# A two-block transformer forward pass: the wait for the last x tile ahead of GpSimd's constant loads is taken out

## What is computed

```python
def hybrid_layer(x, layer_idx, w_in, w_s, b_s, a_ln_g, ...):
    h = jnp.einsum('bsd,de->bse', x, w_in)
    ...
    out_a = gmlp_mixer(a_u, a_v, w_s, b_s, a_ln_g, a_ln_b)
    lam = (jnp.exp(jnp.sum(lam_q1 * lam_k1)) - jnp.exp(jnp.sum(lam_q2 * lam_k2)) + lam_init)
    out_b = diff_attention(b_q, b_k, b_v, lam, lam_init, subln_g)
    out_c = dsa_attention(c_q, c_k, c_v, i_q, i_k, i_w)
    ...

def hybrid_layer_2(x, c, w_ada, b_ada, ...):
    mod = jax.nn.silu(c) @ w_ada + b_ada
    ...
```

## Time and profile before

| | |
|---|---|
| median of three runs (3083.93 to 3088.55) | 3087.78 us |
| time of the profiled execution | 3087.78 us |
| its span, first to last instruction | 3086.0 us |
| outside the span | 1.78 us |
| TensorE busy | 2963.2 us, 96% |
| granted TensorE clock, mean over the span | 0.987 |

### The profile page before, as it was taken

The page is one execution under the profiler, slowest core; times in us unless marked ns, Lnnn a source line. Parts: engine busy times, 40 slices in busy tenths (PEclk is TensorE's granted clock), DMA queues, the critical chain, the costliest instruction groups (busy, mean ns, idle before and its releaser), DMA issues.

```text
span 3086.0 us, 33232 instructions
## 1 busy us (share of the span) xinstructions
PE 2963.2 (96%) x13502; PEld 2200.6 (71%) x13509; DVE 1339.8 (43%) x2012; ACT 631.8 (20%) x1056; POOL 1388.8 (45%) x814
## 2 busy tenths in 40 slices
PE   9999989889999999999999889999998999999997
PEld 5444447467888888888888556667667888887886
DVE  0699957636432236243406652112214422334233
ACT  1501046512010001111301561101112211111111
POOL 2000000055666657656677004344445666566653
PEclk9999999999999999999999999999999999999998
DMA  4011146132332333433433002342333333333331
GB/s 114 21 41 41 34 118 171 56 139 88 96 107 92 103 96 92 128 94 96 123 90 95 1 1 62 82 140 77 83 113 92 95 97 95 96 96 123 94 98 61
DMA packets 364919, 273.22 MB, mean 89 GB/s; under 512 B 14048, under 2 KB 334816, under 8 KB 364768
## 3 DMA queue, kind: packets, MB, share of 16 engines
q1 hardware_dynamic: 357568, 253.30, 28.3%
q10 hardware_dynamic: 4720, 10.68, 0.9%
q0 software_dynamic: 2480, 7.13, 0.9%
HBM read 262.59 MB, written 8.49 MB: 88 GB/s over the span
## 4 chain that ended last, share of the span: by engine, by line
PE 88%; DVE 4%; DMA 3%; issue 2%; POOL 2%; ACT 1%; SPq 0%; DVEq 0%; ACTq 0%; POOLq 0%
PE PS L811 39%; PE PS L823 25%; PE PS L763 5%; PE PS L777 4%; PE PS L446 3%; DMA ring<-in_w_in 2%; PE PS L1015 2%; PE PS L883 2%; PE PS L464 2%; PE PS L484 2%; POOL w_low L1885 1%; PE PS L476 1%; PE PS L897 1%; DVE arena L552 1%; PE PS L978 1%
## 5 line engine op out<-in xcount | busy, mean ns | idle before, releaser
L1885 POOL TENSOR_TENSOR w_low<-ring,w_high 128x1024 fp32r<-128x1024 f32 x382 | 938.1, 2456 | 31.8
L1882 POOL TENSOR_SCALAR w_high<-ring 128x1024 fp32r<-128x1024 f32 x382 | 425.4, 1114 | 1023.4 <-PE PS L823 369.8
L823 PE MATMUL PS<-w_high,hid_high 128*128 128x512 f32 x864 | 337.2, 390 | 9.1 <-issue 9.1
L823 PE MATMUL PS<-w_high,hid_low 128*128 128x512 f32 x864 | 336.8, 390 | 0.0
L823 PE MATMUL PS<-w_low,hid_high 128*128 128x512 f32 x864 | 336.7, 390 | 0.0
L811 PE MATMUL PS<-hT_high,w_high 128*128 128x512 f32 x656 | 272.5, 415 | 14.3 <-POOL w_low L1885 14.3
L811 PE MATMUL PS<-x1T_high,w_high 128*128 128x512 f32 x704 | 275.1, 391 | 3.5 <-DVE x1T_low L1576 3.5
L811 PE MATMUL PS<-x1T_low,w_high 128*128 128x512 f32 x704 | 274.5, 390 | 0.0
L811 PE MATMUL PS<-x1T_high,w_low 128*128 128x512 f32 x704 | 274.4, 390 | 0.0
L811 PE MATMUL PS<-hT_high,w_low 128*128 128x512 f32 x656 | 257.5, 392 | 0.0
L811 PE MATMUL PS<-hT_low,w_high 128*128 128x512 f32 x656 | 257.2, 392 | 0.0
(11 more groups left out here) (268 smaller groups left out, 4602.0 us busy)
## 6 DMA issues: line engine op xcount, KB each, us to landing
ring<-in_w_ff SPq DMA_DIRECT2D x128, 512.0 KB, 3.8
ring<-in_w_in SPq DMA_DIRECT2D x112, 512.0 KB, 3.8
ring<-in_w_gu SPq DMA_DIRECT2D x88, 512.0 KB, 3.8
ring<-in_w_ada SPq DMA_DIRECT2D x48, 512.0 KB, 5.1
ring<-in_w_down SPq DMA_DIRECT2D x44, 512.0 KB, 3.5
ring<-in_w_out SPq DMA_DIRECT2D x32, 512.0 KB, 4.4
ring<-in_w_branch SPq DMA_DIRECT2D x16, 512.0 KB, 3.9
arena<-in_x SPq DMA_DIRECT2D x8, 512.0 KB, 6.8
```

The lines of the kernel that those rows point to most:

```text
L823: mm = pe.matmul(PS[:, 2 * p + half, :], x[:, k, at], w[:, q, half_of(half)], start=(first and n == 0), stop=(last and n == 2))
L1882: pool.tensor_scalar(w_high[:, q, :], ring[:, s, :], 1.0, 1.0, ALU.mult, ALU.mult).then_inc(weights_high, 1)
L1885: pool.tensor_tensor(w_low[:, q, :], ring[:, s, :], w_high[:, q, :].bitcast(F32), ALU.subtract).then_inc(weights_used[s], 1)
```

## The change

One line goes: GpSimd no longer waits for the last tile of x before it issues the constant loads. No transfer is added, dropped or resized, and their order on each queue stays.

```diff
@@ -1911,7 +1911,6 @@
                                pattern=[[-1, P]], channel_multiplier=1).then_inc(ident_made, 1)
             pool.iota(dist, pattern=[[-1, S]], base=S - P, channel_multiplier=1,
                       allow_small_or_imprecise_dtypes=True).then_inc(dist_made, 1)
-            pool.wait_ge(x_loaded[NB - 1], 16)
             load(c_col[:, :], column("c_2"))
             load(b_ada[:, :], column("b_ada_2"))
             for dst, name in ((g_mix_pre, "g_mix_pre_2"), (g_ff_pre, "g_ff_pre_2"), (g_mix_post, "g_mix_post_2"),
```

## The result

The changed kernel took 3107.57 us (median of 4 runs, 3106.03 to 3108.56); the kernel before, in 4 runs, 3088.16 (3083.93 to 3088.87). The ratio is 1.0065 with a 95% interval of 1.0048 to 1.0083: slower by 15 to 26 us; the medians differ by 19.4. The forecast was 3091.5, with a range up to 3096. The profiled execution of the changed kernel took 3105.51 us, its span is 3103.8.

What follows compares the result with a forecast made beforehand. The prediction took the start to be bound by DMA, x's last tile and the first w_in chunk. 0 for earlier constants plus 3.7 us for later x and chunk, on 3087.8, gave 3091.5 us, range 3085.5 to 3096.

Steps and rivals of the forecast that it cites:

- What bounds the kernel: Start of idx on TensorE: bound by DMA, x's last tile with no slack, first w_in chunk with 0.77 us.
- the constants were no prize: Constants complete 11 us sooner in the first 35 us: worth 0 us, at most 4.0 if the cover were gone.
- the price of the contention: Constant packets beside x at the start: x loses the 3.7 us they take, so idx begins 3.7 us later.
- small packets that block an engine for longer than their own time: Sign of error for the DMA engines at the start, named without a size or chance.
- bytes that come too late and cost little: Second batch at the start: issued up to 16 us, landing some 5 us later, when x should be in.
- Rival B: Pile-up of later constants on x and the w_in chunk: up to 9.3 us lost, 3097.1 us; chance 0.13.
- Its point of decision: Pile-up at the w_in chunk: decides from 6.2 us of delay, when about half the second batch gets ahead.
- Rival A: Small packets overlap with x's at the start, x's last tile lands near 13.8: 0 to 1 us; chance 0.22.
- Rival C: TensorE slow when idx starts after longer pauses between tiles: 1 to 2 us more, 3093; no separate chance.
- one for one: After idx everything hangs on TensorE, so a late start is carried to the end in full, within 2 us.
- Rival D: TensorE's low-clock stretches shift onto idle time: faster by over 0.2%, 3081 with four such stretches; chance 0.03.
- turns of the queues at packet boundaries: DMA engines at the start: q0's 184 packets, 11.5 per engine, each go ahead of x, 3.7 us without overlap.

Runs made afterwards that it cites:

- Run 7: Kernel before, but GpSimd waits for the first chunk of w_in, not the last tile of x, before the constant loads: 3089.25 us, ratio 1.0001.
- run 1: Changed kernel with the wait for x's eighth tile put after the ten single-element loads, so only these run early: 3100.08 us, ratio 1.0041.
- run 11: Kernel before, but the load of b_ada (6144 single elements) goes ahead of the wait for x, all other constants behind it: 3093.97 us, ratio 1.0016.
- run 2: Changed kernel with the seven row copies first, then the wait for x, then the other loads: 3099.13 us, ratio 1.0035.
- run 10: As run 2, but each early row copy reads 128 different rows of x instead of one row 128 times: 3091.14 us, ratio 0.9994.
- run 13: As run 4, but the row copies read 128 different rows of x each: 3091.21 us, idx begins at 17.27 us, single execution.
- run 14: As run 4, but gmlp_w_s (256 KB) waits for the first chunk of w_in: 3097.49 us, idx begins at 20.36 us, single execution.
- run 4: Changed kernel, but the ten element loads read the same bytes as contiguous runs per partition: 3098.40 us, ratio 1.0031.
- run 6: Changed kernel, but GpSimd waits until VectorE has made the four biases (7.4 us) before all constant loads: 3097.00 us, ratio 1.0022.
- run 15: As run 6, but the seven row copies and gmlp_w_s wait for the w_in chunk: 3100.30 us, idx begins at 20.80 us, single execution.
- run 9: Changed kernel with element loads as contiguous runs, and row copies and gmlp_w_s waiting for the first w_in chunk: 3090.33 us, ratio 1.0007.
- run 8: Kernel before plus one wait: TensorE begins idx only when all 17 constants have landed: 3109.72 us, ratio 1.0071.
- run 5: Changed kernel, but GpSimd waits for the fourth tile of x before the constant loads: 3091.72 us, ratio 1.0005.

## Why the prediction was wrong

**What bounds the kernel** held: the last tile of x and the chunk with its 0.77 us of slack were the two transfers to watch, and the constants were no prize. Run 7 issues them 2.45 us later at no cost, and the changed kernel has them 3.7 us earlier at no gain.

**The step that failed** is the price of the contention, "each us that q0's packets take is lost to x, 3.7 us by 13.81". The term was mis-sized in kind. A packet's recorded time is not what it takes from its neighbour. In run 1, with elements alone, q0's share is 9.1% from 3 to 22 us, 1.7 us of the engines, while x lost 7.8; in the changed kernel it is 20.1% from 4 to 22 us, 3.6 us with the row copies in it, while x lost 8.6: from 12 to 16 us x's own packets took 0.49 us each, against 0.15. The price that fits runs 1 and 11 goes by single elements, an estimated 9 to 10 ns of an engine each. The 184 packets that I counted hold up to 64 elements each (a load of 1024 elements is 16 packets of 256 bytes in the trace), so up to 0.6 us at that price, where their record says 0.3 on average. The prediction named this case, small packets that block an engine for longer than their own time, as a sign of being wrong, but gave it no price and no chance of its own.

**The second failure** was that the row copies were left out of the forecast, as bytes that come too late and cost little. They came late, but x and the chunk were late too. Runs 2 and 10 show what they cost beyond their size, by the landing of the eighth tile: 4.9 x 16 / 896 = 87 ns of an engine for a repeated row, 1.65 x 16 / 896 = 29 ns for one of different rows (the spread of 0.95 us is 17 ns here). Runs 13 and 14 show the same for the chunk: beside contiguous loads, repeated rows were worth 4.8 us there by run 13 and at most 4.0 by run 14, and gmlp_w_s 1.7.

**Rival B** had the right mechanism, the pile-up behind a first delay, and 0.13 of the chance; but its ceiling of 9.3 us was made from the same recorded times, and the start came 14.24 late. Its point of decision, that the chunk is overtaken by the second batch, is seen in run 4, where x is less than 1 us late and the chunk 6.25. In run 6 the chunk is overtaken too, but run 15 gives about half of that to the single elements. **Rival A** fell for single elements (run 1), but is right for contiguous runs (run 9). **Rival C**, a slow TensorE, was put at 1 to 2 us, left out of the sum, and measured 2.9. The carry of **one for one** held within the spread (run 8). **Rival D** did not show.

The rule of the Trainium skill that the prediction weighed, turns of the queues at packet boundaries ("DMA: Bandwidth & Descriptors", "Queues, rings and completion order"), agrees in direction: q0's packets do get in ahead of queued ones of x. By recorded times it gave 3.7 us, and the measurement decides against that size. The same page of the Trainium skill says, under "Why small descriptors are slow (HBM only)", that each packet has a fixed overhead and that each DMA operation carries a fixed 32 bytes of descriptors. Run 4 agrees in direction: the same bytes in 128 runs per load instead of single elements take x's delay from 8.6 us to below 1. No run separates these parts.

Open: why a repeated row is so dear. The runs show that it is so on two queues and not for different rows; whether the memory or something on the way serialises the reads was not measured. Open too is whether a single element costs its 9 to 10 ns by its reading, its writing or its descriptor, and whether it would on another queue than GpSimd's.

## What to carry to other kernels

A start that is bound by DMA, as this one, is no place for small transfers, even of a few KB: count the separate pieces that they read, not their bytes and not their recorded time, and look whether a source row is read many times. A wait that holds idle work back can be what keeps a queue clean; ask what the freed transfers meet, and where the next link of the chain stands in the queue behind. If constants must come early, lay them out so that each partition reads one run, and keep row copies until the transfers on the path have landed. Here even that gained nothing: run 9 is at 1.0007 (0.9998 to 1.0016), and no variant was faster than the kernel before by more than its interval.

## What else the runs showed of the hardware

TensorE's granted clock after pauses. Where TensorE idled 1.41 us ahead of "idx" and about 1 us at most between tiles (before, runs 7, 9, 10), and 1.62 us ahead of them in run 13, it stood at 1.00 and the 96 matmuls took 41.44 us. With 1.92 us ahead of them (run 5) it was 0.63 from 16 to 20 us and they took 43.13; with 6.23 us (changed, where the clock had fallen at 16 us already) 44.35, with 8.84 (run 6) 44.29, with 17.75 (run 8) 43.54. In these runs a pause at the start costs up to 2.9 us on top of itself, and 2.1 when it is almost three times as long. Run 11 paused 3.55 us between two tiles, fell to 0.74 from 16 to 20 us, and was back in time: 41.44.

VectorE and GpSimd. While GpSimd issued the load of b_ada, one bias of VectorE (L1387) took 2.23 us instead of 0.62, and b_ada's issue 2.73 instead of 2.24. The Trainium skill ("SBUF — State Buffer", "Who interferes with whom") has this as an exclusive lock of a shared port; the trace agrees in that both suffer. It cost nothing here, since neither is on the path, and run 6 without it lost 8.5 us all the same.
